# Prompt attention with seven single score banks, one value bank, and both high halves on the scalar engine

## The reference

```python
z = jnp.einsum('bqhd,bkhd->bhqk', qb, kb) * scale + bias
mask = kpos[None, :] < qpos[:, None]
log_beta = jax.nn.log_sigmoid(z)
log_keep = jnp.where(mask, log_beta - z, 0.0)
rest = lax.cumsum(log_keep, axis=3, reverse=True) - log_keep
a = jnp.where(mask, jnp.exp(log_beta + rest), 0.0)
outs.append(jnp.einsum('bhqk,bkhd->bqhd', a, vb))
```

## Time and profile before

| | us |
|---|---|
| median of three runs | 3411.04 (3404.86 to 3411.8) |
| the profiled execution | 3409.84 |
| its span, first to last instruction | 3408.1 |
| prompt attention, 2045 to 2440 of the span | 395 |
| PE, DVE, ACT busy in that stretch | 326.5, 333.2, 300.3 |

### The profile page before, as it was taken

The page is one execution under the profiler, slowest core; times in us unless marked ns, Lnnn a source line. Parts: engine busy times, 40 slices in busy tenths (PEclk is TensorE's granted clock), DMA queues, the critical chain, the costliest instruction groups (busy, mean ns, idle before and its releaser), DMA issues. The chain is left out here.

```text
span 3408.1 us, 53119 instructions
## 1 busy us (share of the span) xinstructions
PE 3157.8 (93%) x19792; PEld 2621.2 (77%) x19792; DVE 1938.8 (57%) x3310; ACT 936.2 (27%) x1630; POOL 454.0 (13%) x263
## 2 busy tenths in 40 slices
PE   6889999999999997988888978888799999999998
PEld 3369999999987797655555554444598999999996
DVE  4574555555554132666666657888538555555555
ACT  2050000000012021444444437777523000000003
POOL 2011222222112111000000000000202211122210
PEclk9989999999999997999999998999999999999999
DMA  8911111111112212999999971000201111111101
GB/s 326 345 44 37 50 43 49 49 49 43 32 37 79 81 53 101 380 393 399 395 397 398 407 305 44 19 26 13 62 13 50 44 38 36 37 49 43 49 25 53
DMA packets 209560, 434.22 MB, mean 127 GB/s; under 512 B 13648, under 2 KB 112121, under 8 KB 209353
## 3 DMA queue, kind: packets, MB, share of 16 engines
q1 hardware_dynamic: 209089, 430.62, 34.7%
q0 software_dynamic: 272, 1.05, 0.1%
HBM read 417.92 MB, written 13.92 MB: 127 GB/s over the span
## 5 line engine op out<-in xcount | busy, mean ns | idle before, releaser
L73 PE MATMUL bank<-hi,mlp_uphi 128*128 128x364 f32 (+1 forms) x1536 | 510.8, 333 | 15.9 <-DVE lo L228 6.1
L74 PE MATMUL bank<-lo,mlp_uphi 128*128 128x364 f32 (+1 forms) x1536 | 508.2, 331 | 0.0
L75 PE MATMUL bank<-hi,mlp_uplo 128*128 128x364 f32 (+1 forms) x1536 | 507.9, 331 | 0.0
L73 PE MATMUL bank<-mlp_fhi,mlp_dnhi 128*128 128x364 f32 (+1 forms) x1536 | 506.8, 330 | 0.6 <-DVE mlp_flo L373 0.6
L74 PE MATMUL bank<-mlp_flo,mlp_dnhi 128*128 128x364 f32 (+1 forms) x1536 | 504.7, 329 | 0.0
L75 PE MATMUL bank<-mlp_fhi,mlp_dnlo 128*128 128x364 f32 (+1 forms) x1536 | 504.6, 328 | 0.0
L101 DVE SCALAR_TENSOR_TENSOR x_t<-bank,mod,x_t 128x364 f32<-128x364 f32 (+1 forms) x408 | 231.8, 571 | 366.3 <-PE bank L75 364.6
L1656 PE MATMUL bank<-ident,sa_kraw 128*128 128x128 f32 x2048 | 276.2, 279 | 62.5 <-DMA sa_kraw<-in_cache_k 58.7
L1656 PEld LDWEIGHTS bank<-ident,sa_kraw 128*128 128x128 f32 x2048 | 222.9, 141 | 116.6 <-DMA sa_kraw<-in_cache_k 88.0
L73 PEld LDWEIGHTS bank<-hi,mlp_uphi 128*128 128x128 f32 x1536 | 291.7, 190 | 19.7 <-issue 17.7
L1538 DVE COPY sa_kt<-bank 128x512 f32<-128x512 f32 x256 | 177.0, 692 | 216.5 <-PE bank L1656 212.5
(11 more groups left out here) (264 smaller groups left out, 5124.6 us busy)
## 6 DMA issues: line engine op xcount, KB each, us to landing
sa_kraw<-in_cache_k SPq DMA_DIRECT2D x256, 512.0 KB, 10.6
sa_vpage<-in_cache_v SPq DMA_DIRECT2D x256, 512.0 KB, 9.7
en_ring<-in_w_ada SPq DMA_DIRECT2D x96, 512.0 KB, 9.0
mlp_raw<-in_w_up SPq DMA_DIRECT2D x64, 512.0 KB, 4.1
mlp_raw<-in_w_down SPq DMA_DIRECT2D x64, 512.0 KB, 3.6
kv_raw<-in_w_kv SPq DMA_DIRECT2D x16, 512.0 KB, 4.2
en_xrows<-in_x_prompt SPq DMA_DIRECT2D x4, 1024.0 KB, 10.7
out_k_prompt<-kv_stage SPq DMA_DIRECT2D x16, 256.0 KB, 2.1
```

The costliest lines, as they stand in the source:

```text
L73: pe.matmul(out, w_hi, x_hi, start=start, stop=False, skip_group_check=True)
L74: pe.matmul(out, w_hi, x_lo, start=False, stop=False, skip_group_check=True)
L75: return pe.matmul(out, w_lo, x_hi, start=False, stop=stop, skip_group_check=True)
```

## The change

- Seven PSUM banks are used in turn by single heads, and Z of a head waits for the one head that used its bank seven units before (`bank`, `bank_free`); C waits for Z of its own head.
- The V sums have one bank, bank 7. At the end of a half ACT copies it to SBUF (`clear_sum`, tile `pa_o`), after V of the half's last tile, and V of the next half's first tile waits for that copy. `clear_sum` for step i-2 stands at the end of ACT's round i. The high and low halves of the sums are then made from the SBUF copy, the high one a round earlier than before.
- Both H are made by ACT, and in its round they stand behind both E and in front of both L.

```diff
@@ -1758,18 +1759,21 @@
         v_odd = k.at("pa_v1", [P, 8, P], F32, o + 49152)
         cap = k.at("pa_cap", [P, 512], F32, o + 53248)
         c_run = k.at("pa_crun", [P, 2, 2, 512], F32, o + 55296)
+        o_f = k.at("pa_o", [P, 512], F32, o + 63488)
 
         v_rows = [k.at("pa_v0", [P, 8, P], F32, k.HH_AT + 7 * T * 4), v_odd]
         k_rows = k.at("pa_k", [P, 8, P], F32, k.HH_AT + NC * T * 4 + 7 * T * 4)
         (made, sample_kept, zeroed, z_done, clamped, e_done, l_done, c_done, hi_done, lo_done, tri_done, att_done,
-         pv_done, o_hi, o_kept, turned, k_kept, k_in, hi_by_act) = sems(
+         pv_done, o_out, o_hi, o_kept, turned, k_kept, k_in) = sems(
             ctx, nc, "pa", "made", "sample_kept", "zeroed", "z_done", "clamped", "e_done", "l_done", "c_done",
-            "hi_done", "lo_done", "tri_done", "att_done", "pv_done", "o_hi", "o_kept", "turned", "k_kept", "k_in",
-            "hi_by_act")
+            "hi_done", "lo_done", "tri_done", "att_done", "pv_done", "o_out", "o_hi", "o_kept", "turned", "k_kept", "k_in")
         v_in = sems(ctx, nc, "pa", "v_in0", "v_in1")
         block = ctx.enter_context(nc.Block())
-        SLOTS = [(k.ps[0], k.ps[1]), (k.ps[2], k.ps[3]), (k.ps[4], k.ps[5])]
-        ACC = [k.ps[6], k.ps[7]]
+        SLOTS = 7
+        ACC = k.ps[7]
+
+        def bank(x, h):
+            return k.ps[(2 * x.i + h) % SLOTS]
 
 ...
@@ -1840,13 +1844,13 @@
                 act.wait_ge(tri_done, 2 * x.n + h + 1)
 ...
-                act.activation(att[:, x.n % 2, h, 0:x.w], SLOTS[x.i % 3][h][:, 0:x.w], ACT.Exp).then_inc(att_done, 1)
+                act.activation(att[:, x.n % 2, h, 0:x.w], bank(x, h)[:, 0:x.w], ACT.Exp).then_inc(att_done, 1)
 
             def exponential(x, h):
                 act.wait_ge(clamped, 2 * x.n + h + 1)
                 if x.n >= 2:
                     act.wait_ge(c_done, 2 * (x.n - 2) + h + 1)
-                act.activation(t[:, x.n % 2, h, 0:x.w], SLOTS[x.i % 3][h][:, 0:x.w], ACT.Exp).then_inc(e_done, 1)
+                act.activation(t[:, x.n % 2, h, 0:x.w], bank(x, h)[:, 0:x.w], ACT.Exp).then_inc(e_done, 1)
 
             def logarithm(x, h):
                 act.wait_ge(e_done, 2 * x.n + h + 1)
@@ -1857,14 +1861,20 @@
                 if x.n >= 2:
                     act.wait_ge(tri_done, 2 * (x.n - 2) + h + 1)
                 act.activation(c_hi[:, x.n % 3, h, x.lo:512], c_run[:, x.h % 2, h, x.lo:512], ACT.Copy
-                               ).then_inc(hi_by_act, 1)
+                               ).then_inc(hi_done, 1)
+
+            def clear_sum(x):
+                act.wait_ge(pv_done, x.n + 1)
+                if x.h:
+                    act.wait_ge(o_kept, x.h)
+                act.activation(o_f[:, :], ACC[:, :], ACT.Copy).then_inc(o_out, 1)
 
             for i in range(N + 5):
                 if i < N and steps[i].turn:
                     x = steps[i]
                     for h in range(2):
                         act.wait_ge(turned, 2 * x.pair + h + 1)
-                        act.activation(k_t[:, x.pair % 2, 512 * h:512 * h + 512], SLOTS[x.i % 3][h][:, :], ACT.Copy
+                        act.activation(k_t[:, x.pair % 2, 512 * h:512 * h + 512], bank(x, h)[:, :], ACT.Copy
                                        ).then_inc(k_kept, 1)
                 now, before, old = tile_at(i), tile_at(i - 1), tile_at(i - 2)
                 for h in range(2):
@@ -1872,15 +1882,17 @@
                         weights(old, h)
                     if now:
                         exponential(now, h)
+                if before:
+                    high_half(before, 0)
+                    high_half(before, 1)
                 if now:
                     logarithm(now, 0)
-                if before:
-                    high_half(before, 1)
-                if now:
                     logarithm(now, 1)
-                if (x := tile_at(i - 4)) and x.last:
-                    act.wait_ge(pv_done, x.n + 1)
-                    act.activation(k.hi[:, x.pair, columns(x)], ACC[x.h % 2][:, :], ACT.Copy).then_inc(o_hi, 1)
+                if old and old.last:
+                    clear_sum(old)
+                if (x := tile_at(i - 3)) and x.last:
+                    act.wait_ge(o_out, x.h + 1)
+                    act.activation(k.hi[:, x.pair, columns(x)], o_f[:, :], ACT.Copy).then_inc(o_hi, 1)
 
         @block.vector
         def _(dve):
@@ -1892,9 +1904,9 @@
             for i in range(N + 5):
                 if x := tile_at(i):
                     for h in range(2):
-                        z = SLOTS[x.i % 3][h][:, 0:x.w]
+                        z = bank(x, h)[:, 0:x.w]
                         b = k.bias_all[:, 2 * x.pair + h:2 * x.pair + h + 1]
-                        dve.wait_ge(z_done, x.n + 1)
+                        dve.wait_ge(z_done, 2 * x.n + h + 1)
                         if x.diag:
                             dve.scalar_tensor_tensor(out=z, in0=z, scalar=b, in1=cap[:, 0:x.w], op0=ALU.add, op1=ALU.min
                                                      ).then_inc(clamped, 1)
@@ -1909,57 +1921,53 @@
                         else:
                             dve.wait_ge(lo_done, 2 * (x.n - 1) + h + 1)
                         dve.tensor_tensor(c, c, t[:, x.n % 2, h, 0:x.w], ALU.add).then_inc(c_done, 1)
-                    dve.wait_ge(c_done, 2 * x.n + 1)
-                    if x.n >= 2:
-                        dve.wait_ge(tri_done, 2 * (x.n - 2) + 1)
-                    dve.tensor_copy(c_hi[:, x.n % 3, 0, x.lo:512], c_run[:, x.h % 2, 0, x.lo:512]).then_inc(hi_done, 1)
                     for h in range(2):
-                        dve.wait_ge((hi_done, hi_by_act)[h], x.n + 1)
+                        dve.wait_ge(hi_done, 2 * x.n + h + 1)
                         dve.tensor_tensor(c_lo[:, x.n % 3, h, x.lo:512], c_run[:, x.h % 2, h, x.lo:512],
                                           c_hi[:, x.n % 3, h, x.lo:512].bitcast(F32), ALU.subtract).then_inc(lo_done, 1)
                 if (x := tile_at(i - 4)) and x.last:
                     dve.wait_ge(o_hi, x.h + 1)
-                    dve.tensor_tensor(k.lo[:, x.pair, columns(x)], ACC[x.h % 2][:, :],
+                    dve.tensor_tensor(k.lo[:, x.pair, columns(x)], o_f[:, :],
                                       k.hi[:, x.pair, columns(x)].bitcast(F32), ALU.subtract).then_inc(o_kept, 1)
 
         @block.tensor
         def _(pe):
-            def slot_free(i):
-                if i < 3:
+            def bank_free(x, h):
+                unit = 2 * x.i + h - SLOTS
+                if unit < 0:
                     return
-                before = steps[i - 3]
+                before, g = steps[unit // 2], unit % 2
                 if before.turn:
-                    pe.wait_ge(k_kept, 2 * before.pair + 2)
+                    pe.wait_ge(k_kept, 2 * before.pair + g + 1)
                 else:
-                    pe.wait_ge(att_done, 2 * before.n + 2)
+                    pe.wait_ge(att_done, 2 * before.n + g + 1)
 
             def scores(i):
                 if i < N and steps[i].turn:
                     x = steps[i]
                     pe.wait_ge(k_in, 16 * x.pair + 16)
-                    slot_free(i)
                     for h in range(2):
+                        bank_free(x, h)
                         for c in range(4):
-                            last = pe.transpose(SLOTS[i % 3][h][:, c * P:(c + 1) * P], k_rows[:, 4 * h + c, :],
+                            last = pe.transpose(bank(x, h)[:, c * P:(c + 1) * P], k_rows[:, 4 * h + c, :],
                                                 k.ident[:, :])
                         last.then_inc(turned, 1)
                 if x := tile_at(i):
                     if x.n % 12 == 0:
                         pe.wait_ge(k_kept, 2 * x.pair + 2)
-                    slot_free(i)
                     for h in range(2):
+                        bank_free(x, h)
                         rows = slice(64 * h, 64 * h + 64)
-                        last = pe.matmul(SLOTS[i % 3][h][:, 0:x.w], k_t[rows, x.pair % 2, P * x.j:P * x.j + P],
-                                         k.q_t[rows, x.pair, 512 * x.half + x.lo:512 * x.half + 512], start=True,
-                                         stop=False, skip_group_check=True)
-                    last.then_inc(z_done, 1)
+                        pe.matmul(bank(x, h)[:, 0:x.w], k_t[rows, x.pair % 2, P * x.j:P * x.j + P],
+                                  k.q_t[rows, x.pair, 512 * x.half + x.lo:512 * x.half + 512], start=True,
+                                  stop=False, skip_group_check=True).then_inc(z_done, 1)
 
             scores(0)
             scores(1)
             for i in range(N + 3):
                 if x := tile_at(i - 1):
                     for h in range(2):
-                        z = SLOTS[x.i % 3][h]
+                        z = bank(x, h)
                         pe.wait_ge(lo_done, 2 * x.n + h + 1)
                         for half in (c_hi, c_lo):
```

(6 more changed lines are left out.)

## The result

The changed kernel takes 3440.14 us (median of four runs, 3437.6 to 3442.37), the kernel before 3411.27 on the same chips: a ratio of 1.0095 (95% interval 1.0082 to 1.0107). It is slower by 29 us; 27 were forecast. Its profiled span is 3439.7, by 31.6 more than before, and all of it lies in the prompt attention: from the first T to the last T are 31.6 us more.

What follows compares the result with a forecast made beforehand. No engine is full; the loop through the engines that closes last sets the time. +3.0 a pair in eight pairs is +24, the end copy +0.7, the clock +2: 27, so 3437 us; range 3418 to 3454.

Steps and rivals of the forecast that it cites:

- Both H on ACT: Full tiles: H of head 0 stands behind W, E, W, E; four steps take 17.8 against 16.3, +1.5 a pair.
- the rival in which DVE was the bound: Prompt attention: DVE's time decides, so freeing it of 34.1 us of CASTs gives 3395; chance 0.07.
- The copy of the sums: Half starts: ACT's copy waits for V before the next W; 4.25 and 4.05 against 2.65, +3.0 a pair.
- The rival in which V is done in time: Half starts: the copy never waits for V, a pair is 48.5, the end about 3414, no change; chance 0.08.
- The turn: From T of h to T of i: earlier C and a shorter way to D, -0.8 a pair in seven pairs.
- C now starts when the first head's Z is done, half of 1.13 earlier: Between tiles h and i: C no longer waits for both heads' Z and starts 0.55 earlier.
- The seven banks give nothing elsewhere: Outside h to i: no gain from the banks, since the first W after T decides and Z is done by then.
- The ramps: The five remaining steps, into c, d, e, g and h: 18.0 instead of 18.7, -0.7 a pair.
- The clock: PE's clock dips lengthen T to W, now in the loop: two dips in all pairs, +2; upper end 16.
- gaps in front of T leave the clock at the 2.4 GHz level but for two dips: PE's idle gaps: 1.7 us before T left whole pairs at 1.00, so only two dips, each costing 1.
- The first rival: PE idles around each copy of the sums, so its clock falls twice a pair: +16, 3451; chance 0.15.
- The sum: Prompt attention: +3.0 a pair, 51.0 instead of 48.0; eight pairs give +24.

Runs made afterwards that it cites:

- H alone: The kernel before with only H changed: both made by ACT, in front of the logarithms; 3425.35 us, ratio 1.0052.
- low later: The kernel before with DVE's low half of the sums made one round later; 3402.67 us, ratio 0.9981.

## Why the prediction was right

The size was right, 27 forecast and 29 measured (31.6 between the profiled executions, from which the forecast counts), by the two terms that were forecast to carry it. Each step that the forecast counted from H to H:

- *Both H on ACT.* Forecast 4.62, 4.62, 4.22, 4.33; measured 4.57, 4.59, 4.24, 4.33. The experiment with H alone shows 4.59 without any other part of the change, and a program that is 0.52% slower. DVE, 34 us of work lighter, waits longer, 95.7 us for H: the rival in which DVE was the bound is refuted.
- *The copy of the sums.* Forecast 4.25 and 4.05; measured 4.26 and 4.04. Forecast waits of 1.4, measured 1.59 and 1.38, 23.4 in all. Over all sixteen starts T to T grew by 23.7 (forecast 24), and moving the copy takes 23.5 of that back. The rival in which V is done in time is refuted: ACT waits in front of all sixteen copies. The two parts add up, as the forecast had them do: at a clock of 1.00 a middle pair is 2.0 longer with the banks and the copy and H as before, 1.2 with H alone and 3.3 with both.
- *The turn.* Forecast -0.8, measured -0.43 from T to T: a term that was mis-sized. The step that failed is "C now starts when the first head's Z is done, half of 1.13 earlier": the two heads' Z end together, and the wait by heads gives 0.04 where 0.55 was forecast. What is left is the shorter way from A to D, 0.28 with H alone where 0.2 was forecast, and an earlier Z, 2.61 after T of h where it was 2.75. The kernel with late sums and H as before, which has the seven banks, has this Z too, and H alone hasn't: it fits a Z that waits for one head's W and no longer for both, so "The seven banks give nothing elsewhere" was 0.15 short here.
- *The ramps.* Forecast 3.45, 3.4, 4.1, 3.45 and 3.6; at the high clock measured 3.44, 3.40, 4.11, 3.44 and 3.56.
- *The clock.* Forecast +2, two dips that cost 1 each, with 16 as the end. In the profile of the changed kernel the clock falls about tile c in seven of eight pairs, in two of them for longer than in the others, and these pairs are 0.5 to 1.9 longer than at the high clock, 6.6 together: the price of a dip was about right, their number was mis-sized. (PE idles 8.9 us of 51.8 a pair, where 11 were forecast.) The kernel with added work on PE puts the whole at 5 to 8. The step that failed is the reading that gaps in front of T leave the clock at the 2.4 GHz level but for two dips. It came from a pair at 1.00; in the kernel before the clock was low at tile c too, in the first four pairs. Tile c of the third and of the fifth pair there:

```profile
2156.00:2158.00 2.00, 2.00 (x8) 1.96 (x8) 1.56 (x5) 1.24 (x4) 0.00 (x0) 0.50 0.00 0
...
2252.00:2254.00 2.00, 1.72 (x12) 1.14 (x11) 1.56 (x5) 1.47 (x5) 0.00 (x0) 1.00 0.00 0
```

From c to d both pairs take 4.38, as DVE's wait for the sums closes that step (low later). The first rival's mechanism is real, at less than half its price: one dip a pair, at tile c, and none in the second half. The experiment shows that work in the gap takes the loss away; which amount of idling lets the clock fall, it doesn't show.

The sum took eight equal pairs. At the high clock, in the kernel with added work on PE, a middle pair is 3.3 longer than before (51.30 against 47.98), six times; the first pair of the changed kernel is 2.3 longer, for no copy stands in front of its first half, and the last 2.7 (45.11 against 42.40). That is 25.0, where 24 was forecast: what the turn doesn't give, the first and the last pair don't cost, and that these cancel is luck. The other 6.6 of the 31.6 us between the profiles are the clock's.

## What to carry to other kernels

Where no engine is full, find the loop through the engines that closes last and count in it, handoff by handoff, from the rows: here that gave single steps within 0.05 us, except for the turn. A copy moved off the busiest engine can cost time when its new place puts it behind instructions that its own loop releases, as H here behind W and E, and an instruction that waits costs everything that stands behind it in the list: the same copy one round later was free. Then look for what waits in front of the loop on the engines that seem to have time: DVE's work on sums that nobody needed soon, one round later, made the kernel before 0.19% faster.

## What the runs showed of the hardware

- Z of two heads, 64 partitions each, four matmuls of 0.64 us, took 1.13 together. Two of them, one of each head, start at 2237.15 and two at 2237.68, within 0.01 of each other, and a wait for the first head alone gained 0.04: as far as the runs show, matmuls on different halves of the rows run side by side.
- Matmuls that repeat a result made the program 5 to 8 us faster, by holding the granted clock at 1.00 through a gap in front of a loop's matmuls. In a kernel where another wait stood at the same place (the kernel before, c to d 4.38 at the low and at the high level) the low clock cost nothing.
